# Rotary embedding of two attentions of the second block: the swap of halves by VectorE's shuffle in place of a TensorE product

## The reference, cut to what matters

```python
h = _rmsnorm(x, norm_g[l])
z = einsum('bsd,de->bse', h, w_in[l])            # q, k, v and a gate for A, B, C and D
q_a, k_a = _rmsnorm(q_a, qn_a[l]), _rmsnorm(k_a, kn_a[l])
q_a, k_a = _axial_rope(q_a, row, col), _axial_rope(k_a, row, col)   # two ropes of 32 features: A
q_b, k_b = _rope_2(q_b, t), _rope_2(k_b, t)                         # one rope of 64 features: B
q_d, k_d = _rope_2(q_d, t), _rope_2(k_d, t)                         # ropes of 32 features: D
mix = concatenate([o_a * silu(g_a), o_b * silu(g_b), o_c * silu(g_c), o_d * silu(g_d)])
x = x + einsum('bsm,md->bsd', mix, w_out[l])

def _rope_2(x, pos):                              # half = d // 2
    x1, x2 = x[..., :half], x[..., half:]
    return concatenate([x1 * cos - x2 * sin, x2 * cos + x1 * sin], axis=-1)
```

## Time and profile before

| | |
|---|---|
| runs | 1442.4 us median (1438.07, 1442.4, 1443.17) |
| profiled execution | 1442.34 us, its span 1440.5 us |
| granted TensorE clock, mean | 0.985 of full speed |
| TensorE busy | 1364.4 us, 95% |
| VectorE busy | 874.4 us, 61% |
| ScalarE busy | 733.5 us, 51% |
| GpSimd busy | 383.6 us, 27% |

### The profile page before, as it was taken

How to read it: one execution, slowest core, us unless ns; L and a number is a source line. 1 busy time by engine, 2 the same in 40 slices (tenths; PEclk the granted TensorE clock), 3 DMA queues, 4 the chain that set the end, 5 groups by cost and what they waited for, 6 DMA issues and landing times.

```text
span 1440.5 us, 19833 instructions
## 1 busy us (share of the span) xinstructions
PE 1364.4 (95%) x7342; PEld 1056.5 (73%) x7342; DVE 874.4 (61%) x1519; ACT 733.5 (51%) x1561; POOL 383.6 (27%) x273
## 2 busy tenths in 40 slices
PE   7999999999899999999998899999899999999897
PEld 6867788777787678787776776776666877675665
DVE  6667545557653663555577675568656665578555
ACT  5556455655145464656554464446444554546443
POOL 2232221355121332224553122421111111421111
PEclk9999999999999999999999999999999999999999
DMA  7423541226253122112266341621314433411311
GB/s 255 99 51 109 122 99 48 67 77 234 73 161 75 45 88 61 61 45 66 89 237 175 103 91 42 124 72 40 116 54 91 112 91 72 111 59 23 118 52 59
DMA packets 185669, 135.64 MB, mean 94 GB/s; under 512 B 91366, under 2 KB 166758, under 8 KB 185318
## 3 DMA queue, kind: packets, MB, share of 16 engines
q1 hardware_dynamic: 181638, 119.17, 30.7%
q10 hardware_dynamic: 3936, 15.21, 2.7%
HBM read 122.03 MB, written 12.32 MB: 93 GB/s over the span
## 4 chain that ended last, share of the span: by engine, by line
PE 70%; DVE 15%; ACT 7%; issue 2%; POOL 2%; DMA 1%; SPq 1%; ACTq 0%; DVEq 0%; POOLq 0%
PE pb L1657 18%; PE pb L1659 17%; PE pb L1658 17%; PE pb L1748 5%; PE pb L1697 5%; PE pb L1724 5%; ACT prob L1803 3%; ACT tmp L1803 2%; DVE wl L2182 2%; DVE prob L2452 2%; SPq L2728 1%; PE pb L1778 1%; POOL wl L2596 1%; ACT wh L1823 1%; DMA tbias<-zscr 1%
## 5 line engine op out<-in xcount | busy, mean ns | idle before, releaser
L2596 POOL TENSOR_TENSOR wl<-wr,wh 128x512 fp32r<-128x512 f32 x178 | 253.2, 1423 | 705.8 <-ACT wh L1823 701.5
L1657 PE MATMUL pb<-xh,wl 128*128 128x512 f32 (+1 forms) x864 | 347.3, 402 | 19.2 <-DVE wl L2182 15.9
L1659 PE MATMUL pb<-xh,wh 128*128 128x512 f32 (+1 forms) x864 | 322.2, 373 | 0.0
L1658 PE MATMUL pb<-xl,wh 128*128 128x512 f32 (+1 forms) x864 | 321.7, 372 | 0.0
L2182 DVE TENSOR_TENSOR wl<-wr,wh 128x512 fp32r<-128x512 f32 x208 | 164.6, 794 | 163.6 <-ACT wh L1823 163.3
L1823 ACT CAST wh<-wr 128x512 fp32r<-128x512 f32 (+1 forms) x386 | 220.3, 605 | 41.5 <-PE pb L1659 23.5
L1657 PEld LDWEIGHTS pb<-xh,wl 128*128 128x128 f32 x864 | 164.1, 190 | 73.4 <-issue 39.1
L1659 PEld LDWEIGHTS pb<-xh,wh 128*128 128x128 f32 x864 | 163.8, 190 | 29.8
L1658 PEld LDWEIGHTS pb<-xl,wh 128*128 128x128 f32 x864 | 164.7, 191 | 25.5 <-issue 4.3
L1657 PE MATMUL pb<-wh,xl 128*128 128x256 f32 (+1 forms) x320 | 110.1, 344 | 15.0 <-DVE wl L2182 12.3
L2066 ACT COPY prob<-pb 128x512 f32<-128x512 f32 (+3 forms) x128 | 61.4, 480 | 111.4 <-PE pb L1724 111.0
(11 more groups left out here) (201 smaller groups left out, 2336.6 us busy)
## 6 DMA issues: line engine op xcount, KB each, us to landing
wr<-w_in SPq DMA_DIRECT2D x39, 1024.0 KB, 5.4
wr<-w_out SPq DMA_DIRECT2D x14, 1024.0 KB, 5.2
wr<-w_in SPq DMA_DIRECT2D x52, 256.0 KB, 4.6
wr<-w_branch SPq DMA_DIRECT2D x48, 128.0 KB, 2.3
x<-prob SPq DMA_DIRECT2D x12, 512.0 KB, 3.6
wr<-w_mem_kv SPq DMA_DIRECT2D x4, 1024.0 KB, 5.8
prob<-x ACTq DMA_DIRECT2D x2, 2048.0 KB, 11.0
wr<-w_out SPq DMA_DIRECT2D x16, 256.0 KB, 4.3
```

What stands on the lines that cost most here:

```text
L1657: e.matmul(ps, ll, rh, start=start, stop=False)
L1658: e.matmul(ps, lh, rl, start=False, stop=False)
L1659: t = e.matmul(ps, lh, rh, start=False, stop=stop)
L2596: t = e.tensor_tensor(wl[:, j % 2, c0:c1], wr[:, j % 2, c0:c1], wh[:, j % 2, c0:c1].bitcast(F32), ALU.subtract)
```

## The change

In A and D the product with `rot16` is left out. VectorE's `stream_shuffle` swaps the halves inside each group of 32 rows (`HALVES`), straight from the buffer into a second one, as soon as ScalarE's `pair` is done; the sign moves into the sine table. The product with the sine table then reads two SBUF operands, where it read PSUM and SBUF. The step no longer takes a PSUM bank and is counted as no TensorE time. It stands sooner in the list: for A behind 2, 6 and 2 feature blocks in place of 6, 10 and 3 (`qsquares` stays where it was), for D behind 1 in place of 3. B is not changed.

```diff
-            rows_s.append(np.sin(ang))
+            rows_s.append(-np.sin(ang) if d == 32 and r % 32 < 16 else np.sin(ang))
...
-    if k in ("dqk", "squares", "rope1", "rope2", "qsquares", "dsquares"):
+    if k in ("dqk", "squares", "rope1", "qsquares", "dsquares") or k == "rope2" and s["br"] == "B":
         return 860
...
     def behind(n, l, br, tm, sq):
-        for _ in range((6, 10, 3)[n] if br == "A" else 3):
+        for _ in range({"A": (2, 6, 2)[n], "B": 3, "D": 1}[br]):
             yield
-        b, t2 = GR[0].take(), None if br == "A" else TM.take()
+        b, t2 = GR[0].take() if br == "B" else None, None if br == "A" else TM.take()
         put("rope2", l=l, br=br, n=n, src=tm, b=b, tm=t2)
-        give(b, *[t2] * (br != "A"))
+        give(*[b] * (br == "B"), *[t2] * (br != "A"))
         if br == "A":
+            for _ in range((4, 4, 1)[n]):
+                yield
             b = GR[0].take()
             put("qsquares", l=l, n=n, b=b, sq=sq)
...
+    HALVES = [(j + 16) % 32 for j in range(32)]
...
-            elif k == "rope2":
+            elif k == "rope2" and s["br"] == "B":
...
-                t = e.matmul(bank(b), C(ROT[s["br"]][0]), tm(s["src"]), start=True, stop=True)
+                t = e.matmul(bank(b), C("rot32"), tm(s["src"]), start=True, stop=True)
...
-                w.wait_ge(aux, aux.at(b))
...
-                e.tensor_tensor(t2, bank(b), tabs[:, 1, :], ALU.mult).then_inc(v_fn.sem, v_fn.mark(ends=(b,)))
+                if br == "B":
+                    w.wait_ge(aux, aux.at(b))
+                    e.tensor_tensor(t2, bank(b), tabs[:, 1, :], ALU.mult).then_inc(v_fn.sem, v_fn.mark(ends=(b,)))
+                else:
+                    w.wait_ge(a_copy, a_copy.at(("pair", s["src"])))
+                    e.stream_shuffle(t2, src, HALVES).then_inc(v_fn.sem, v_fn.mark())
+                    w.wait_ge(v_fn, v_fn.n)
+                    e.tensor_tensor(t2, t2, tabs[:, 1, :], ALU.mult).then_inc(v_fn.sem, v_fn.mark())
```

More of the change, by code:

```diff
@@ L147 @@
     tensor_tensor_reduce = tensor_reduce = tensor_tensor_scan = reciprocal = memset = op
-    bn_stats = bn_aggr = dma_start = op
+    bn_stats = bn_aggr = dma_start = stream_shuffle = op
 class Waits:
@@ L1456, in build @@
     biases = [setB[:, 3072:3968], setA[:, 4096:4992], tbias[:, 0, :], tbias[:, 1, :]]
-    ROT = {"A": ("rot16", 0), "B": ("rot32", 2), "D": ("rot16", 4)}
+    TABLE = {"A": 0, "B": 2, "D": 4}
+    HALVES = [(j + 16) % 32 for j in range(32)]
     SCALE = {"mla": float(96 ** -0.5)}
@@ L2714, in sync_program @@
                 for q in range(2):
-                    t = e.dma_start(tabs[:, q, :], a["tables"][ROT[br][1] + q])
+                    t = e.dma_start(tabs[:, q, :], a["tables"][TABLE[br] + q])
                     t.then_inc(d_tab.sem, d_tab.mark((l, br)))
```

## The result

The changed kernel takes 1448.57 us (median of 5 runs, 1447.49 to 1450.61) against 1441.73 us: ratio 1.0048, interval 1.0036 to 1.0059. So it lost some 7 us where 5 won were forecast, and the time lies outside the range. The profiled execution took 1449.69 us, its span is 1447.9 us at a mean granted clock of 0.982 (the earlier trace rows belong to a span of 1440.5 us at 0.985).

The account below looks back on a forecast made before the run. TensorE was taken as the bound, busy 95% of the span. Of 10.3 us removed, waits for VectorE left 0.4 us in A and 2.1 in D per layer: 5.0 us won, 1442.3 to 1437.3 us, range 1431.5 to 1444.

Parts of the forecast that it names:

- What is removed: In A and D, 12 rotation products of 0.86 us leave TensorE, 10.3 us, all on the path.
- The shuffle: On VectorE, one more instruction in each of the 12 rotations, taken at 0.72 us.
- The slow rival: Shuffle passes four groups of rows one after another, 2.4 us each: 13.2 us more, 1450.5 us; chance 0.07.
- The sine product: On VectorE, with two SBUF operands, each of 12 can be held by a GpSimd cast, up to some 1.0 us.
- A: the wait: In A's product for n = 2, TensorE waits 1.9 us per layer for VectorE's second weight chunk.
- the 0.2 us at A's first product: TensorE's wait there for the last product of VectorE's queue, booked at 0.2 us, between 0 and 0.9.
- D: the step that failed: In D VectorE has room; 2.58 us less a 0.5 us wait wins 2.1 us per layer.
- The one tight place is n = 2: In D, that rotation stands between two copies of transposed probabilities; the second copy is done 4.8 us behind its transposes' start.
- The wait of 0.5 us at the product with the values: In D, TensorE waits about 0.5 us (0 to 1.2) for the second copy of transposed probabilities.
- Everything behind these stretches is released by TensorE's own progress: Behind the changed stretches of A and D, everything moves along with TensorE, loads included; no size given.
- A wait's price: In A and D, TensorE's waits were subtracted at their own length: 1.9, 0.2 and 0.5 us per layer.

Follow-up runs that it names:

- e8: The original kernel with its rotation products kept on TensorE, but the rotations at the places of e7: 1441.16 us, ratio 0.9999.
- e7: The changed kernel with A's rotations of n = 0 and 1 ahead of A's first weight chunk and D's at their old place: 1429.32 us, ratio 0.9924.
- e3: The changed kernel with only D's rotation steps back in their old places, A's staying sooner: 1436.06 us, ratio 0.9964.
- e6: The original kernel with five dependent VectorE instructions more ahead of `u`, once in each layer: 1452.58 us, ratio 1.0084.
- e5: The original kernel, products kept on TensorE without shuffle, with the rotations of A and D at the changed kernel's sooner places: 1448.32 us, ratio 1.0058.
- e4: The changed kernel with D's tables in a buffer of their own, loaded right behind A's: 1440.88 us, ratio 0.9998.
- e1: The changed kernel, shuffle kept, with all rotation steps back in their old places: 1433.73 us, ratio 0.9956.
- e2: The changed kernel with only A's rotation steps back in their old places, D's staying sooner: 1447.86 us, ratio 1.0044.

## Why the prediction was wrong, by its own steps

**What is removed: right.** 12 products of 0.86 us were put at 10.3 us. Between e8 and e7, which differ in them alone, lie 0.75% or 10.8 us.

**The shuffle: right.** 0.72 us were taken. After's records (least, median, most in ns):

```profile
L2515 DVE STREAM_SHUFFLE scr<-tmp x6: 718/729/740, 823.6 to 1161.7; 128x512 f32<-128x512 f32 x6
...
L2515 DVE STREAM_SHUFFLE tmp<-tmp x6: 721/742/755, 931.2 to 1275.1; 128x512 f32<-128x512 f32 x6
```

The 0.6 us that were estimated from the Trainium skill (VectorE: DVE Perf Modes, The perf-mode tier table) were 0.13 short. The slow rival, at 2.4 us, had the sign and nearly the time (1450.5 us) by luck, by a mechanism that isn't there; its 13.2 us were counted from 0.6 us, and from the 0.72 of the sum they are some 12.

**The sine product: right in kind, small in size.** It answers to the earlier trace rows:

```profile
L2517 DVE TENSOR_TENSOR scr<-scr,tabs x6: 692/694/1082, 824.4 to 1162.4; 128x512 f32<-128x512 f32 x6
L2517 DVE TENSOR_TENSOR tmp<-tmp,tabs x6: 691/692/693, 932.0 to 1275.9; 128x512 f32<-128x512 f32 x6
...
1145.51 1.08 DVE L2517 TENSOR_TENSOR scr<-scr,tabs 128x512 f32<-128x512 f32 x1
```

Two of twelve were held, for 0.39 us each: the first of A in either layer, at 824.39 and 1145.51 us, as forecast. With the rule of the Trainium skill (SBUF — State Buffer, Who interferes with whom) this agrees: GpSimd had a cast running from 823.64 and from 1144.76 us, and the other ten met no GpSimd instruction.

**A: the wait right, its price short.** 1.9 us per layer were forecast for the chunk, 2.17 came; the 0.2 us at A's first product did not. What the sum lacked is the half clock behind it, 1.6 to 1.8 us per layer by the account above. e3 is this A with D at its old place, and its 1436.06 us lie 1.2 us from the 1437.3 forecast, but by the profiled runs that is in good part luck. Matched with before product by product, e3's trace wins only 0.2 us from ahead of A to behind D in the first layer and 1.8 in the second, 2.0 of the 5.0 forecast. The other 4 us of the profiled runs lie where the change does nothing: 2.0 us ahead of A, with a wait for a weight chunk in the first block (3.53 us at 786 us in before, 1.93 at 785 in e3), and 2.1 us behind the second layer's D, where before has two lowered stretches (one at 1341 us, 0.57, one at 1368 us, 0.66) and e3 none at the same work (1.00). The first of the two, in before and in e3:

```profile
1341.00:1345.00 4.00, 3.18 (x15) 3.21 (x16) 3.62 (x8) 1.10 (x2) 0.12 (x1) 0.57 0.71 173
...
1337.00:1341.00 4.00, 3.02 (x25) 2.90 (x26) 3.97 (x8) 1.11 (x2) 0.28 (x1) 1.00 0.65 181
```

**D: the step that failed.** "VectorE has room here, and the chunks that stand behind the rotations of n = 0 and 1 belong to tiles whose products come later. The one tight place is n = 2." The chunk does come in time. What also stands behind the rotation of n = 0 is `u`, and what stands ahead of it is D's table; of tables the prediction looks at A's and at SyncE's place for B's. The rotation of D was moved past a transfer that I did not look up. The trace of before had enough to see it. The two tables are issued from 921.31 on, the second 0.6 us behind the first, and a transfer of a table lands there 3.9 to 5.7 us after its issue; with the longest the second lands at 927.6 (its record: 927.54). A rotation of 2.65 us and the chunk's 0.61 us then put `u` at 930.9, 3.3 us behind its 927.55, at a place where TensorE already waited 0.24 us. Measured: 3.35 us more, 3.59 for 0.24.

The wait of 0.5 us at the product with the values, which was the term of the sum for D, is not there, though the copy was as late as forecast (5.1 us behind the start of its transposes for the 4.8). VectorE's second copy and the product in after:

```profile
957.07 0.42 DVE L2476 COPY prob<-pb 128x256 f32<-128x256 f32 x1
...
956.83 2.38 PE L1751 MATMUL pb<-prob,setB 128*64 128x256 f32 x24
```

The row is two products, one for each half of the queries. The first reads earlier copies, so the row starts with no idle time; the second, which reads this copy (done at 957.49), starts 1.13 us into the row, at 957.96. The prediction took the start of the row for the place where the copy is needed.

**"Everything behind these stretches is released by TensorE's own progress":** of no help for the tables of D. Their issue did move with the rest: it stands in SyncE's queue right behind a weight load, which waits for a GpSimd cast, and came 3.55 us later in after than in before (924.86 for 921.31), as TensorE's work there did (3.5 us in the account). It is not B's last rotation that held it, whose cosine product was over more than 20 us sooner (900.75 us in before, 902.91 in after). But the transfer takes its own 6.2 us from the first issue to the last landing in both kernels, and in after its first reader comes 4 us behind the issue.

**A wait's price.** The sum takes each wait at its own length. By the account, a wait of 2.2 us in A and one of 3.6 us in D each drew a stretch at half clock that took 1.6 to 1.8 us more, and e6 shows the same behind a planted wait. After is 12.1 us slower than e3 (0.84%): 6.8 us are the two waits for `u`, 3.2 us the half clock behind them, and the last 2 us I could not place. The profiled runs of the two differ by 2.6 us already ahead of A, where the change does nothing.

## What to carry to other kernels

Before an instruction is moved forward, list all that it waits for, each transfer with its issue and landing in the trace, and all that stands behind it up to the next instruction for which another engine waits; a load that is early for the old place can be late for the new one. Put added work where the engine is idle and the inputs are there (e7), and not a few steps sooner by feel: the same shuffle won 10.9 us where it was put well and lost 6.9 where it was put in after. A wait on a full TensorE can cost more than its length, since most of those over 2 us here drew a stretch at the slower clock.

## What the runs showed of the hardware that was not expected

- Idle time of TensorE was followed by a stretch at 1.2 GHz in after (2.17 us idle, then 0.70 and 0.87; 3.59 us, then 0.57) and in e6 (2.90 us, then 0.65), but not everywhere: behind e5's 2.01 us the clock stayed, and in e4 the same wait of 2.16 us for A's second chunk was followed by the lower level in the first layer and not in the second. So the length of a wait alone did not decide it. The Trainium skill (TensorE: Matmul & The Clock Gate, Part 1: The HAM clock gate) says that TensorE's clock is halved when the engine has been idle and full again when it has been busy; after and e6 agree with it, e5 and the second layer of e4 do not show it. The stretches of e5 around its wait, and those of e4 behind its two, as above:

```profile
928.00:932.00 4.00, 1.99 (x14) 0.91 (x14) 3.66 (x9) 0.90 (x3) 0.00 (x0) 1.00 0.02 4
932.00:936.00 4.00, 4.00 (x33) 2.91 (x30) 1.60 (x6) 2.64 (x8) 0.43 (x1) 1.00 0.00 0
...
834.00:838.00 4.00, 4.00 (x12) 3.10 (x12) 3.90 (x7) 0.00 (x0) 0.81 (x1) 0.57 0.88 179
1152.00:1156.00 4.00, 4.00 (x18) 3.31 (x19) 3.90 (x6) 1.11 (x2) 0.92 (x1) 1.00 0.87 173
```

- The mean clock of the profiled runs was 0.988 in e1 and e7, 0.985 in before, 0.982 in after, 0.981 in e6. Over all runs it was 0.982 to 0.991 in e1, 0.986 to 0.989 in e7 and 0.982 to 0.988 in before, so the first three can't be told apart by it; after (0.980 to 0.982) and e6 (0.979 to 0.984) lie lower.
- A shuffle is two instructions, the mask's load and the shuffle; the load took 13 to 15 ns in the twelve records of after.
- With the shuffle the wait for a GpSimd chunk ahead of D is longer in the first layer, 1.33 to 1.83 us in e1, e2, e3, e7 and after against 0.45 in before and 0.22 in e5. In the second layer it is not: 0.99 to 1.41 us in the same five against 1.57 in before and 1.80 in e5. Its cause was not tried.
